# Down projections over eight accumulator banks, another step order in the third one, up products grouped by width

## What is computed

```python
merged = (jax.nn.sigmoid(ga) * (out_a @ w_branch_a[l])
          + jax.nn.sigmoid(gb) * (out_b @ w_branch_b[l]))
x = x + merged @ w_out[l]
h2 = rmsnorm(x, norm_ffn[l])
u = h2 @ w_up[l]                                   # 2048 -> 2 * 5632
up = jnp.pad(u, ((0, 0), (1, 1), (0, 0)))
cw = conv_w[l]
u = up[:, :-2] * cw[0] + up[:, 1:-1] * cw[1] + up[:, 2:] * cw[2] + conv_b[l]
gate, val = jnp.split(u, 2, axis=-1)
x = x + (jax.nn.silu(gate) * val) @ w_down[l]      # 5632 -> 2048
```

## Time and profile before

| | us |
|---|---|
| median of 3 runs | 2575.2 (2573.34 to 2577.14) |
| the profiled execution | 2573.78 |
| its span, first to last instruction | 2572.0 |
| TensorE busy in it | 2519.3 (98%) |
| VectorE busy | 1520.6 (59%) |
| ScalarE busy | 1222.3 (48%) |
| mean granted TensorE clock | 0.995 |

### The profile page before, as it was taken

The page is one execution under the profiler, slowest core; times in us unless marked ns, Lnnn a source line. Parts: engine busy times, 40 slices in busy tenths (PEclk is TensorE's granted clock), DMA queues, the critical chain, the costliest instruction groups (busy, mean ns, idle before and its releaser), DMA issues.

```text
span 2572.0 us, 32850 instructions
## 1 busy us (share of the span) xinstructions
PE 2519.3 (98%) x12468; PEld 2115.5 (82%) x12468; DVE 1520.6 (59%) x1755; ACT 1222.3 (48%) x1556; POOL 49.6 (2%) x71
## 2 busy tenths in 40 slices
PE   7999999999999999999999999999899999999997
PEld 6888888878888888888878887788788888888886
DVE  4665655655767467755765346655565565565565
ACT  5444556444665355534544344444544344443443
POOL 0100100000000000000000000000000000000000
PEclk9999999999999999999999999999999999999999
DMA  7555455645555555555547365445465655555553
GB/s 258 193 195 180 147 164 167 227 171 180 182 192 183 195 180 189 177 204 180 187 172 251 118 194 162 156 164 180 140 195 189 188 188 195 181 190 190 185 203 114
DMA packets 249926, 469.96 MB, mean 183 GB/s; under 512 B 22320, under 2 KB 25648, under 8 KB 249184
## 3 DMA queue, kind: packets, MB, share of 16 engines
q1 hardware_dynamic: 249824, 468.58, 55.5%
HBM read 466.42 MB, written 2.13 MB: 182 GB/s over the span
## 4 chain that ended last, share of the span: by engine, by line
PE 96%; DVE 2%; ACT 1%; issue 0%; POOL 0%; DMA 0%; POOLq 0%; DVEq 0%; SPq 0%; ACTq 0%
PE psum L1606 21%; PE psum L1568 19%; PE psum L1570 19%; PE psum L1569 19%; PE psum L1607 10%; PE psum L1610 1%; PE psum L1698 1%; PE psum L1683 1%; PE psum L1619 1%; PE psum L1609 1%; PE psum L1847 1%; PE psum L1668 1%; DVE wl L1025 0%; PE psum L1658 0%; ACT wh L621 0%
## 5 line engine op out<-in xcount | busy, mean ns | idle before, releaser
L1025 DVE TENSOR_TENSOR wl<-raw,wh 128x1024 fp32r<-128x1024 f32 x856 | 1049.1, 1227 | 956.9 <-ACT wh L621 952.2
L621 ACT ACTIVATE wh<-raw 128x1024 fp32r<-128x1024 f32 x856 | 904.3, 1059 | 1041.5 <-PE psum L1570 617.8
L1568 PE MATMUL psum<-wh,ha 128*128 128x512 f32 x1728 | 694.4, 402 | 8.5 <-DVE wl L1025 8.1
L1570 PE MATMUL psum<-wh,ha 128*128 128x512 f32 x1728 | 675.7, 391 | 0.0
L1569 PE MATMUL psum<-wl,ha 128*128 128x512 f32 x1728 | 674.3, 390 | 0.0
L1606 PE MATMUL psum<-ha,wh 128*128 128x512 f32 x1320 | 465.9, 398 | 5.0 <-DVE x_rows L1245 4.5
L1568 PEld LDWEIGHTS psum<-wh,ha 128*128 128x128 f32 x1728 | 325.6, 188 | 75.1 <-issue 10.3
L1570 PEld LDWEIGHTS psum<-wh,ha 128*128 128x128 f32 x1728 | 325.2, 188 | 70.3
L1569 PEld LDWEIGHTS psum<-wl,ha 128*128 128x128 f32 x1728 | 326.0, 189 | 65.2
L1607 PE MATMUL psum<-ha,wl 128*128 128x256 f32 x1320 | 370.1, 280 | 0.0
L1606 PE MATMUL psum<-hb,wh 128*128 128x512 f32 x960 | 339.3, 398 | 5.2 <-DVE rows L1546 3.2
(11 more groups left out here) (215 smaller groups left out, 1393.1 us busy)
## 6 DMA issues: line engine op xcount, KB each, us to landing
raw<-in_w_up SPq DMA_DIRECT2D x152, 1024.0 KB, 5.0
raw<-in_w_in SPq DMA_DIRECT2D x120, 1024.0 KB, 5.1
raw<-in_w_down SPq DMA_DIRECT2D x108, 1024.0 KB, 4.9
raw<-in_w_out SPq DMA_DIRECT2D x32, 1024.0 KB, 5.0
raw<-in_w_branch_a SPq DMA_DIRECT2D x8, 1024.0 KB, 5.0
raw<-in_w_branch_b SPq DMA_DIRECT2D x8, 1024.0 KB, 5.0
x_rows<-in_x SPq DMA_DIRECT2D x4, 512.0 KB, 8.8
bias<-in_b_rpb SPq DMA_DIRECT2D x32, 64.0 KB, 7.0
```

The source lines that it names most:

```text
L621: act.activation(wh[q % SPLIT_SLOTS][:], raw[q // 2 % RAW_SLOTS][:, 2 * (q % 2):2 * (q % 2) + 2, :], ACT.Copy).then_inc(hi_done, 1)
L1025: dve.tensor_tensor(wl[q % SPLIT_SLOTS][:], raw[q // 2 % RAW_SLOTS][:, 2 * (q % 2):2 * (q % 2) + 2, :], wh[q % SPLIT_SLOTS][:].bitcast(F32 ...
L1568: pe.matmul(acc, hi, wh[s][:, c, :], start=first and c == 0, stop=False)
L1570: ins = pe.matmul(acc, lo, wh[s][:, c, :], start=False, stop=last and c == 1)
```

## The change

Five things are done.

1. The down projections of passes 0 and 1 of the first part, and of all four of the second, spread their four row blocks over all eight banks (`row_bank`: block b in banks 2b and 2b+1), and wait for the last channel read-out only ahead of block 2. The channel blocks behind them start once the banks 0 to 3 are free, and wait for the other two read-outs only ahead of `v=1`.
2. The last row block of the projection out goes to banks 6 and 7, and the last two fills of that input to banks 4 and 5 (`fill_bank`), so that `first_pair` starts when the read-out before the last is done.
3. The last two `merged` fills move from ahead of the projection out to behind its second step, and their splits behind the third `ahead`.
4. The row of roots moves from behind the eighth step of `first_pair` to behind the seventh, in both parts.
5. The third down projection takes its steps in the order `LAST_DOWN1`: four steps of block 0, four of block 1, then the last two of each, then blocks 2 and 3. Loads, splits, read-outs and the fills of the next input follow that order. In every channel step the four wide matmuls of a chunk now come together, and then the four narrow ones (the last chunk narrow first).

The loops over row blocks that had four of them are written out in full.

```diff
+LAST_DOWN1 = [(b, j) for half in (range(4), range(4, 6)) for b in range(2) for j in half]
+LAST_DOWN1 += [(b, j) for b in (2, 3) for j in range(6)]
+LAST_DOWN1_ENDS = [LAST_DOWN1.index((b, 5)) for b in range(4)]
+LAST_DOWN1_ENTER = [11, 13, 19]
...
+    def row_bank(g):
+        for first in R_DOWN1[:2] + R_DOWN2:
+            if first <= g < first + 4:
+                return 2 * (g - first)
+        return 6 if g == R_OUT1 + 3 else 2 * (g % 2)
...
+    def fill_bank(F):
+        return 4 + F % 2 if F in (T_FFN1 + 6, T_FFN1 + 7) else 4 + F % 4
...
-                for d in range(4):
-                    acc = psum[:, 4 * v + d, :]
-                    hi, lo = (w[s][:, c, P * d:P * d + P] for w in (wh, wl))
-                    if k < KC - 1:
-                        pe.matmul(acc, hi, both, start=k == 0, stop=False)
-                        ins = pe.matmul(acc[:, 0:SEQ], lo, src[:, k, 0, :], start=False, stop=False)
...
+                def wide(stop):
+                    for d in range(4):
+                        ins = pe.matmul(psum[:, 4 * v + d, :], wh[s][:, c, P * d:P * d + P], both,
+                                        start=k == 0, stop=stop)
+                    return ins
+
+                def narrow():
+                    for d in range(4):
+                        ins = pe.matmul(psum[:, 4 * v + d, 0:SEQ], wl[s][:, c, P * d:P * d + P], src[:, k, 0, :],
+                                        start=False, stop=False)
+                    return ins
+
+                if k < KC - 1:
+                    wide(False)
+                    ins = narrow()
+                else:
+                    narrow()
+                    ins = wide(True)
...
-        pe.wait_ge(sem["merge_rows"], 4)
-        for f in range(2):
-            transposes(T_MERGE + 6 + f, lambda c, t: merged[1][:, t, (2 * f + c) * P:(2 * f + c + 1) * P])
-        row_blocks(S_OUT1, R_OUT1, 4, 8, hb, split_by(T_MERGE), extra=next_input(T_FFN1, R_OUT1))
+        enter_ffn1 = next_input(T_FFN1, R_OUT1)
+
+        def out1_hook(b, j):
+            if b == 0 and j == 1:
+                pe.wait_ge(sem["merge_rows"], 4)
+                for f in range(2):
+                    transposes(T_MERGE + 6 + f, lambda c, t: merged[1][:, t, (2 * f + c) * P:(2 * f + c + 1) * P])
+            if b == 2 and j == 7:
+                pe.wait_ge(sem["tr_lo"], T_FFN1 + 4)
+            enter_ffn1(b, j)
+
+        row_blocks(S_OUT1, R_OUT1, 4, 8, hb, split_by(T_MERGE), extra=out1_hook)
 
         def channel_blocks(step0, c0, n, src, rows_before):
 
-            pe.wait_ge(row_free, FREE + rows_before)
+            pe.wait_ge(row_free, FREE + rows_before - 2)
             with pe.Fori(0, n) as i:
                 for v in range(2):
                     pe.wait_ge(chan_free, FREE + c0 + v - 1 + 2 * i)
+                    if v:
+                        pe.wait_ge(row_free, FREE + rows_before)
                     for j in range(8):
                         channel_step(step0 + 8 * v + j, i, 2, v, j, src)
...
-            row_of_roots(count)
+                if j == 6:
+                    row_of_roots(count)
             pe.wait_ge(sem["rstd_row_ok"], count)
+            pe.wait_ge(row_free, FREE + rows_before)
             pe.wait_ge(chan_free, FREE + c0)
...
+            if p < 2:
+                for b in range(4):
+                    g = R_DOWN1[p] + b
+                    pe.wait_ge(row_free, g + 1)
+                    if b == 2:
+                        pe.wait_ge(chan_free, FREE + C_UP1[p] + 2 * n)
+                    for j in range(8):
+                        hb_by(j0, 4)(j)
+                        rows_step(S_DOWN1[p] + 8 * b + j, 0, 0, hb, (2 * j, 2 * j + 1), g, j == 0, j == 7)
             rows_before = R_DOWN1[p] + 4
+
+        for s, (b, j) in enumerate(LAST_DOWN1):
+            g = R_DOWN1[2] + b
+            if j == 0:
+                pe.wait_ge(row_free, g + 1)
+            hb_by(8, 4)(j)
+            rows_step(S_DOWN1[2] + s, 0, 0, hb, (2 * j, 2 * j + 1), g, j == 0, j == 5)
+            if s in LAST_DOWN1_ENTER:
+                c = LAST_DOWN1_ENTER.index(s)
+                if c == 0:
+                    pe.wait_ge(chan_free, FREE + 22)
+                pe.wait_ge(row_free, FREE + R_DOWN1[2] + c + 1)
+                x_group(T_MIX2, c)
```

More of the change, by code:

```diff
@@ L790, in _ @@
                     ins.then_inc(sem["sig_done"], 1)
[L791 to L792 removed]
+        enter_ffn1 = next_input(1, T_FFN1, "ffn1", R_OUT1)
+        def out1_hook(b, j):
+            if b == 0 and j == 2:
+                merged_hi(3)
+            enter_ffn1(b, j)
+        row_blocks(S_OUT1, R_OUT1, 4, 8, no_evac, extra=out1_hook)
         def row_of_roots(count):
@@ L846, in tail @@
                         up1_stage(p, stage, 1, j0 + n - 1, n - 1)
-                if p == 2:
-                    enter(b, j)
-            row_blocks(S_DOWN1[p], R_DOWN1[p], 4, 2 * n, no_evac, extra=tail)
+            if p < 2:
+                row_blocks(S_DOWN1[p], R_DOWN1[p], 4, 8, no_evac, extra=tail)
+            else:
+                for s, (b, j) in enumerate(LAST_DOWN1):
+                    ahead(S_DOWN1[p] + s)
+                    tail(b, j)
+                    if s - 1 in LAST_DOWN1_ENTER:
+                        group_hi(ha, T_MIX2, LAST_DOWN1_ENTER.index(s - 1), "mix2")
+                    if s - 3 in LAST_DOWN1_ENTER:
+                        c = LAST_DOWN1_ENTER.index(s - 3)
+                        act.wait_ge(row_free, FREE + R_DOWN1[p] + c + 1)
+                        sum_squares(2, x_rows, c)
         def pair(bank, n=2 * SEQ, rows=P):
@@ L1252, in enter_ffn1 @@
         def enter_ffn1(b, j):
+            if b == 0 and j == 2:
+                merged_lo(3)
             if b and j == 3:
@@ L1321, in tail @@
                         up1_stage(p, stage, 1, j0 + n - 1, n - 1)
-                if p == 2 and b and j == 3:
-                    group_lo(ha, T_MIX2, b - 1, "mix2")
-            row_blocks(S_DOWN1[p], R_DOWN1[p], 4, 2 * n, add_rows(x_rows), extra=tail)
+            if p < 2:
+                row_blocks(S_DOWN1[p], R_DOWN1[p], 4, 8, add_rows(x_rows), extra=tail)
+            else:
+                for s, (b, j) in enumerate(LAST_DOWN1):
+                    ahead(S_DOWN1[p] + s)
+                    tail(b, j)
+                    if s - 2 in LAST_DOWN1_ENTER:
+                        group_lo(ha, T_MIX2, LAST_DOWN1_ENTER.index(s - 2), "mix2")
+                    if s in LAST_DOWN1_ENDS:
+                        add_rows(x_rows)(b, R_DOWN1[p] + b, S_DOWN1[p] + s + 1, 0, 0)
         p16 = cmp_p[:].rearrange("p h t n -> p (h t) n")
@@ L1987, in _ @@
             pe.wait_ge(chan_free, FREE + C_UP2[p] + 3)
-            row_blocks(S_DOWN2[p], R_DOWN2[p], 4, 8, ha, hb_by(11 + 4 * p, 4))
+            for b in range(4):
+                g = R_DOWN2[p] + b
+                pe.wait_ge(row_free, g + 1)
+                if b == 2:
+                    pe.wait_ge(chan_free, FREE + C_UP2[p] + 4)
+                for j in range(8):
+                    hb_by(11 + 4 * p, 4)(j)
+                    rows_step(S_DOWN2[p] + 8 * b + j, 0, 0, ha, (2 * j, 2 * j + 1), g, j == 0, j == 7)
             rows_before = R_DOWN2[p] + 4
```

52 lines of the change are left out of this document (25 added, 27 removed).

## The result

The changed kernel takes 2553.8 us (median of 4 runs, 2552.65 to 2554.16), the kernel before 2575.1 in the same comparison: ratio 0.9918, 95% interval 0.9906 to 0.9930. It is 21 us faster. The time lies inside the stated range, 11 us above the forecast of 2543, in the place that the prediction gave to groups that bring little, plus a fall of the clock. The profiled execution took 2554.16 us, its span is 2552.4, against 2573.78 and 2572.0.

A forecast was written before the change was run, and what follows sets the result against it. TensorE, 98% busy, was taken as the bound. Terms 9.3 + 1.55 + 4.4 + 6.0 + 0.7 - 1.65 + 11.7 = 32.0 us off the profiled 2573.8 gave 2541.8, forecast as 2543 us at the median; range 2535 to 2557.

The forecast's parts named there:

- groups that bring little: Rival for the channel steps: half of the grouping's 11.7 us lost gives 2549 us, all of it 2555; chance 0.25.
- What bounds the kernel: Whole kernel: TensorE, busy 2519.3 of 2572.0 us, is the bound; only its waits and losses while busy count.
- Down projections over eight banks: Hand-overs from five down projections to channel blocks: a pause of 1.85 us each goes, 9.3 us gained.
- Projection out into the first up projection: Start of the first up projection: the wait for the last read-out goes, 1.55 us gained.
- Merged fills: Ahead of the projection out: the 2.73 us wait and the clock's fall (1.7 us) go, together 4.4 us gained.
- Third down projection: After its first four steps: the 4.27 us wait and 1.7 us for the clock go, 6.0 us gained.
- Row of roots, part one: First pair of part one: the wait for the copied row goes under the eighth step, 0.7 us gained.
- Row of roots, part two: First pair of part two: late diagonal, new wait of 2.3 us, 1.65 us lost; no clock fall counted (up to 1.7).
- Wide and narrow in groups: Channel steps: groups reach the clean rate of 2.773 us everywhere, 0.040 us on about 288 steps, 11.7 us gained.
- The slower rival: Channel steps: narrow matmuls behind narrow ones show their 189 ns loads, 2681 us; sign turns at 0.131 us; chance 0.04.
- The fast rival: Channel steps: narrow matmuls come at 0.113 us in groups, 2531 us; chance 0.10.

The follow-up runs named there:

- eight banks alone: The kernel before with only the down projections spread over eight banks and the weaker wait; 2565.9 us, ratio 0.9963.
- groups alone: The kernel before with only the wide and narrow matmuls of a channel step in groups of four; 2572.2 us, ratio 0.9983.
- alternation put back: The changed kernel with the channel steps' wide and narrow matmuls alternating again, all else still changed; 2557.6 us.
- all matmuls wide: The changed kernel with every narrow matmul of the channel steps taking all 512 columns; 2799.8 us in one run.
- runs of eight: The changed kernel with the 8 wide matmuls of a channel step's two chunks together, then the 8 narrow ones (last step narrow first); 2549.65 us.
- runs of sixteen: The changed kernel with even channel steps 8 wide then 8 narrow, odd steps 8 narrow then 8 wide; 2547.3 us.
- 384 columns: The changed kernel with the narrow matmuls of the channel steps at 384 instead of 256 columns; 2686.1 us in one run.

## Why the prediction was right, and where it was not

**What bounds the kernel** held. TensorE is the bound, and its waits for others, measured from start to start, were worth what was read from them.

**Down projections over eight banks**: forecast 9.3 us, measured 5 x 1.78 = 8.9 in the down stages and the emptied pipeline's 0.1 each in the up stages. Right. No engine took the place of the read-outs; no split is named at a hand-over. What the sum did not have is that the pauses also gave: the fast stretches of the alternating order followed four of them. The two experiments that do one part alone show this in the passes, and alternation without pauses costs 2.824 a step where the prediction read 2.813 as its usual rate. The 2.813 was a mean over sixteen clean steps and 48 slow ones; some 70 of the 304 steps were clean already (four stretches of sixteen and a few in the first pairs), not 16.

**Projection out into the first up projection**: 1.55 forecast, 1.60 measured. **Merged fills**: 4.4 forecast, 4.24 measured. **Third down projection**: 6.0 forecast, 6.03 measured. All three in size and place. The part of the clock in the merged term was luck of the profiled execution, though: with the same wait the clock fell in the profiles of the kernel before and of eight banks alone, not in that of groups alone.

**Row of roots, part one**: no wait is left there, as forecast. The 0.7 us is borne out by two runs that both alternate, eight banks alone with the old place and alternation put back with the new one: the seventh to ninth steps of this pass take 9.55 and 8.86 us together, 0.70 less.

**Row of roots, part two**: the new wait was forecast at 2.3 us and came with 2.1, in the forecast place and by the forecast name. The step that failed is "I take none, the row being nearer": the clock did fall, and the term became 3.1 instead of 1.65 us. The reading that 2.12 us without a fall and 2.6 with one enclose a threshold was too simple. The same 2.58 us stand with and without a fall, and so do the same 2.12 us at the start, the very row that the prediction leaned on. Here it is in the changed kernel and in the run with all matmuls wide, each with the window behind it:

```profile
37.94 0.47 PE L1614 MATMUL psum<-wh,ha 128*128 128x512 f32 x1 [2.15 <-DVE wl L1062]
37.90:41.10 3.20, 3.16 (x14) 1.00 0.54 207
37.84 0.76 PE L1614 MATMUL psum<-wh,ha 128*128 128x512 f32 x1 [2.12 <-DVE wl L1062]
37.90:41.10 3.20, 3.20 (x8) 0.50 0.48 180
```

So the length of a stop alone doesn't decide, and such a term has two values. That it depends on where the stop lies in time is a guess that no run here shows. It was no single bad draw either: behind the wait of 2.0 to 2.2 us for the diagonal the clock fell in all four profiles that have it (changed kernel, alternation put back, runs of eight, runs of sixteen).

**Wide and narrow in groups** is the failed term: 11.7 us forecast. Measured are 3.9 on top of the other parts by the whole time, 5.6 by the up stages, and 1.7 in the passes when done alone. Between the kernel before and the changed one it is 2.1 by the up stages: they are 0.3 us shorter in sum, in which 0.6 of emptied pipelines and 0.7 of the first row of roots were gained and 3.1 of the second lost. The step was "groups cannot be better than the clean rate but reach it everywhere". It took the distance of wide matmuls from row steps, where no narrow one is near, and assumed that a change of width costs only at the change. In fact it costs over the next four or five wide matmuls. In single alternation at its usual rate a return costs 0.0064 us (2.824 - 2.773 over eight), behind four narrow ones 0.017, behind eight or sixteen 0.020. From eight returns of 0.0064 a step went to two of 0.017: 0.051 to 0.033 us. And where alternation had been at its clean rate, where a return costs nothing, the grouped order lost 0.033 us a step. The prediction had seen the wobble and put it at 0.01 to 0.02 us, the right size, but as a bound in place of the term. With it the term would have been two returns of 0.015 a step against 0.040, some 3 us.

**The slower rival** is out: narrow matmuls stand 0.120 us apart in runs of sixteen, below the 0.131 from which it would decide. The rule of the Trainium skill that the prediction set beside it, on the page "TensorE: Matmul & The Clock Gate" (it stands there in the section "The mechanism", ahead of the section that the prediction names), is not borne out here: loads of 189 ns for all 128 rows run beside matmuls that stand 0.120 us apart. The fast rival, 0.113, is out by the same rows: only the first of a run comes so early.

So the sum of the waits was right to about 1 us, 11.7 was 9.6 too high, and the fall of the clock brought 1.4 on top: 2543 + 9.6 + 1.4 is 2554, against 2553.8 measured. Between the two profiled executions the 1.5 us of the untouched stages come in as well: 2541.8 + 9.6 + 1.4 + 1.5 is 2554.3, against 2554.16. The prediction's time came inside the range because the range allowed for groups that bring little, and not because the largest term was right.

## What to carry over

Read the waits of the engine that is the bound from start to start, and look for what each moved piece asks for next: the one late diagonal was visible in the old trace. A rate measured among equal instructions may not hold beside unequal ones; look for the rows just behind a change before you multiply by 300 steps. Where two operand widths share a kernel, make the runs of each long across steps: going from four to sixteen brought 6 us here.

## What the runs showed of the hardware

- A matmul in a run of its own width costs its columns at 2.4 GHz and about 0.013 us: 0.2267 us for 512 and 0.120 for 256 columns. The 0.2267 hold for weights or activations as the stationary operand and with another bank each time.
- Behind a change from 256 to 512 columns the next five matmuls are late by 0.027 us in sum, and the first two behind the change back are early by 0.007; 0.020 us are left, for eight as for sixteen narrow ones. In runs of four 0.017 are left. With 384 columns it is 0.022 (3.244 against 3.200 us a step, two returns). Whether the width or a stream shorter than its load brings it stays open.
- The alternating order has two steady rates, 2.774 and 2.824 us a step. It changes from one to the other at pauses, behind transposes, and where a loop turns. The steps of the grouped order stay at 2.800 to 2.807, but for those where a loop turns (2.784 and 2.816). What makes the difference inside the engine stays open; no run here tells it.
- The clock may fall or not behind the same wait: behind the 2.58 us for `merged` (it fell in the kernel before and with eight banks alone, not with groups alone), behind 2.12 us at the start (it fell with all wide and with 384 columns, not in the kernel before), and behind the same 32 small matmuls in the second block (it fell near 1484 us in the kernel before and at the same place in the changed one, not in four of the variants). A fall of 3.4 us over running matmuls costs 1.7 us. The executions of one kernel differ by 0.6 to 6 us; how much of that is the clock only the profiled ones could tell.
